# The entry of the down product: two first high parts ahead of a square on ScalarE, and one small load first of four on SyncE's queue

## The reference, cut to what matters

```
u = square(relu(rms_norm(x, g_pre_ffn) @ w_up))      # (T, 1024) @ (1024, 4096)
x = x + rms_norm(u @ w_down, g_post_ffn)             # (T, 4096) @ (4096, 1024)
```

## Time and profile before

| | |
|---|---|
| median of 3 executions | 2371.45 us (2370.8 to 2372.8) |
| the profiled execution's own time | 2372.79 us |
| its span | 2370.2 us |
| mean granted clock of TensorE | 0.998 |
| PE busy | 2341.4 us, 99% |
| DVE busy | 1365.5 us, 58% |
| ACT busy | 797.8 us, 34% |
| POOL busy | 481.4 us, 20% |
| DMA moved | 319.18 MB, mean 135 GB/s |

### The profile page before, as it was taken

One profiled execution on the slowest core, in us unless ns is written; L12 is line 12 of the kernel. 1 busy time (PEld: TensorE's weight loads), 2 busy tenths in 40 slices (PEclk: granted clock), 3 DMA queues, 4 the chain that ended last, 5 costly groups with the idle time before them and its releaser, 6 DMA issues.

```text
span 2370.2 us, 36572 instructions
## 1 busy us (share of the span) xinstructions
PE 2341.4 (99%) x14144; PEld 2198.5 (93%) x14144; DVE 1365.5 (58%) x2494; ACT 797.8 (34%) x1484; POOL 481.4 (20%) x732
## 2 busy tenths in 40 slices
PE   8999999999999999999999999999999999999998
PEld 7899999999999999999999999988999998888886
DVE  7425263553376667667666435556755556777675
ACT  5222223323222232222232423333654554332233
POOL 1002120212165456447536000000000000000001
PEclk9999999999999999999999999999999999999999
DMA  5216363653424324423432644223434336533424
GB/s 194 85 41 229 104 224 114 200 170 125 168 71 135 123 80 132 137 93 112 132 118 88 232 134 132 99 89 98 134 123 154 132 125 253 185 116 125 169 71 142
DMA packets 249990, 319.18 MB, mean 135 GB/s; under 512 B 9332, under 2 KB 191480, under 8 KB 249720
## 3 DMA queue, kind: packets, MB, share of 16 engines
q1 hardware_dynamic: 249416, 315.66, 39.2%
q0 software_dynamic: 432, 1.57, 0.4%
HBM read 205.53 MB, written 111.67 MB: 134 GB/s over the span
## 4 chain that ended last, share of the span: by engine, by line
PE 92%; DVE 5%; POOL 1%; issue 1%; DMA 0%; ACT 0%; DVEq 0%; SPq 0%; POOLq 0%; ACTq 0%
PE bank L935 13%; PE bank L937 13%; PE bank L936 13%; PE bank L1050 5%; PE bank L1049 5%; PE bank L1047 5%; PE bank L1327 5%; PE bank L1329 5%; PE bank L1328 5%; PE bank L1181 1%; PE bank L1009 1%; PE bank L1298 1%; PE bank L1011 1%; PE bank L1010 1%; PE bank L1297 1%; PE bank L1296 1%
## 5 line engine op out<-in xcount | busy, mean ns | idle before, releaser
L935 PE MATMUL bank<-XH,WHI 128*128 128x384 f32 x1968 | 674.2, 343 | 2.3 <-issue 1.5
L937 PE MATMUL bank<-XH,WLO 128*128 128x384 f32 x1968 | 659.3, 335 | 0.0
L936 PE MATMUL bank<-XL,WHI 128*128 128x384 f32 x1968 | 658.8, 335 | 0.0
L935 PEld LDWEIGHTS bank<-XH,WHI 128*128 128x128 f32 x1968 | 370.2, 188 | 6.7 <-issue 3.3
L936 PEld LDWEIGHTS bank<-XL,WHI 128*128 128x128 f32 x1968 | 370.4, 188 | 0.8
L937 PEld LDWEIGHTS bank<-XH,WLO 128*128 128x128 f32 x1968 | 369.9, 188 | 0.0
L1393 ACT ACTIVATE ZST<-bank 128x384 f32<-128x384 f32 x204 | 99.9, 491 | 402.8 <-PE bank L937 396.5
L1327 PE MATMUL bank<-WSH,USH 128*128 128x512 f32 x448 | 175.3, 391 | 2.8 <-DVE USL L2397 2.8
L1329 PE MATMUL bank<-WSH,USL 128*128 128x512 f32 x448 | 175.3, 391 | 0.0
L1328 PE MATMUL bank<-WSL,USH 128*128 128x512 f32 x448 | 175.1, 391 | 0.0
L2546 POOL TENSOR_TENSOR ORS<-OMS,mhalf 128x1 f32<-128x1 f32 x108 | 75.2, 697 | 471.7 <-DVE OMS L2071 471.7
(11 more groups left out here) (282 smaller groups left out, 4807.1 us busy)
## 6 DMA issues: line engine op xcount, KB each, us to landing
WRAW<-in_w_in SPq DMA_DIRECT2D x80, 512.0 KB, 4.1
scratch_z<-ZST SPq DMA_DIRECT2D x68, 576.0 KB, 3.3
UOP<-scratch_uq SPq DMA_DIRECT2D x28, 1024.0 KB, 7.3
HZ<-scratch_z SPq DMA_DIRECT2D x32, 576.0 KB, 4.8
WRAW<-in_w_up SPq DMA_DIRECT2D x32, 512.0 KB, 5.2
scratch_uq<-U SPq DMA_DIRECT2D x16, 1024.0 KB, 3.9
WQ<-in_w_down SPq DMA_DIRECT2D x16, 1024.0 KB, 5.1
scratch_uq<-SU SPq DMA_DIRECT2D x16, 768.0 KB, 5.4
```

Source lines behind the costliest of these rows:

```text
L935: pe.matmul(psum[c][:, 0:CH], WHI[p][:, k, :], XH[:, k, s], start=(k == 0), stop=False)
L936: pe.matmul(psum[c][:, 0:CH], WHI[p][:, k, :], XL[:, k, s], start=False, stop=False)
L937: last = pe.matmul(psum[c][:, 0:CH], WLO[p][:, k, :], XH[:, k, s], start=False, stop=(k == KT - 1))
```

## The change

Two orders are changed, and nothing else: no instruction is added or removed.

- SP: `u8_load(0)` is issued ahead of `wq_load(0, 2)`, `wq_load(0, 3)` and `uq_load(2)`, right after the wait for the end of the up product.
- ACT: in the last step of the up product, `up_sq(s, 1)` (a relu and a square) is issued behind `w_hi_part(0)` and `u_hi(0)` instead of ahead of the wait and of both. In the other steps the order stays.

```
@@ -865,10 +865,10 @@
             uq_load(1)
             uq_store(NQ - 2)
             sp.wait_ge(up_mm, 14 * NP)
+            u8_load(0)
             wq_load(0, 2)
             wq_load(0, 3)
             uq_load(2)
-            u8_load(0)
             uq_store(NQ - 1)
             for n in range(3, 7 * NGD):
                 g, i = divmod(n, 7)
@@ -1834,13 +1834,14 @@
                 if nxt:
                     op_hi(s + 1, 3)
                     op_hi(s + 1, 4)
-                up_sq(s, 1)
                 if nxt:
+                    up_sq(s, 1)
                     op_hi(s + 1, 5)
                 else:
                     act.wait_ge(up_mm, 14 * s + 10)
                     w_hi_part(0)
                     u_hi(0)
+                    up_sq(s, 1)
                 take_last(s, ACT.Relu)
                 up_sq(s, 2)
                 up_sq(s, 3)
```

## The result

| | us | of the kernel before |
|---|---|---|
| before, 22 executions | 2371.89 (2368.84 to 2373.89) | 1 |
| changed, 22 executions | 2375.53 (2373.47 to 2379.04) | 1.0015, 95% interval 1.0010 to 1.0021 |
| predicted | 2371.3 (2368.6 to 2373.8) | |

The change costs 3.6 us, which is within the 0.2% of "the same", but its interval is clear of 1, and the time lies above the predicted range. A longer series than the three executions of before tells smaller differences than the 0.2% that I had put down for a measurement.

What follows compares the result with a forecast made beforehand. PE, busy for 2341.4 of 2370.2 us, bounds the kernel. The gaps' - 1.80 + 1.66 = - 0.14 us gave 2372.65 from the profiled 2372.79; set against the median 2371.45, the forecast was 2371.3 us, range 2368.6 to 2373.8.

Steps and rivals of the forecast that it cites:

- What bounds the entry: At the down product's entry, DVE's unbroken queue behind the squares, not the sample columns' load, sets the 2.0 us second gap.
- ScalarE's part and the first gap: On ACT, WSH starts 1.80 us earlier, the squares' end stays at 1997.95, and PE's first gap is 1.80 us shorter.
- Second gap 3.66 us.: PE's wait for U8L between product 0 and the sample columns grows by 1.66 us, from 2.0 to 3.66.
- Quarter 3 lands at 2004.8 ... I take nothing.: The w_down load, moved past by U8R's, lands 1.4 us later, before DVE's quarter sums want it at 2004.92: cost nothing.
- a cover of 0.12 us: Time between quarter 3's forecast landing at 2004.8 and DVE's quarter sums wanting it at 2004.92.
- Rival 2: At DVE's two quarter sums: quarter 3 is late, + 0.2 us to 2371.65, or 2372.65 with sharing; chance 0.27.
- my 1.4 us for 512 KB: Cost to quarter 3 of U8R's load ahead of it, from two loads landing 2.8 us apart for 1 MB.
- Rival 3: Behind PE's longer second gap the clock falls to half pace: + 2.7 us to 2374.0, 2376.8 at the end; chance 0.07.
- The page's slices give PE the full granted clock everywhere: Reading of the profile page before the change: PE has the full granted clock in all slices.
- the rows of gaps up to 2.8 us show no fall.: In the timeline before the change, PE came out of a 2.8 us gap at full pace, 0.229 us per matmul.

## Why the prediction was wrong, point by point

Two steps failed, both terms that the sum put at nothing: the cost of the earlier load to quarter 3 ("I take nothing"), where DVE waited 1.45 us, and the clock in the longer gap, which cost 2.73 us in the profiles. The clock weighs more: with quarter 3 on time, in the kernel with the load in third place, the median is 2.5 us over before.

- **What bounds the entry.** Right: DVE's queue behind the squares, and not the load of the sample columns. U8H was ready 9 us early and no time was won by it.
- **ScalarE's part and the first gap.** Right in each step: 1.84 us for 1.80, squares' end unmoved, DVE idle for 1.64 us for 1.6, sums 0.03 us behind the last square.
- **"Second gap 3.66 us."** Right as a sum for the kernel without the late quarter: 3.75 in the kernel with the load in third place. In the changed kernel 5.27.
- **"Quarter 3 lands at 2004.8 ... I take nothing."** Wrong. In the changed kernel it lands 11.2 us after the last up matmul, 1.6 later than the 9.6 I had, and DVE waits 1.45 us. With a cover of 0.12 us I took the lower end of a cost whose upper end, 0.34, was itself too low: both were worked out from the spacing of two loads in one execution, and left out whatever else passes through the engines. Rival 2 had the mechanism, a wait of DVE for the load; by its bound of 0.34 us it had a quarter of the price, and its upper price, 1 us more for sharing with the stores, came near the 1.45 us by luck, as holding the stores back changed nothing. The price is not one of SyncE's part alone: with ScalarE's old order the same loads land at 9.7 to 9.8, which needs no wait, and this is what my 1.4 us for 512 KB gives.
- **Rival 3, the clock, at a chance of 0.07.** Wrong in the chance, right in the price in the profiles: 2.7 us forecast, 2.73 in the sum and 2.76 by the kernel with the gap filled (1.5 in its medians). I had the row of slow matmuls at the start, and the rule of the Trainium skill, TensorE: Matmul & The Clock Gate, section HAM oscillation, that a long idle stretch sends the array to half clock; the trace agrees, the granted clock being 0.50 behind the 5.27 us gap. I weighed it down because one profile showed no fall behind 2.80 us. At the entry, gaps of 2.80 us were followed by slow matmuls in two of three profiles, one of 2.58 us in the only one, gaps of 3.75 us and more in all seven, and gaps of up to 2.01 us in none.
- **"The page's slices give PE the full granted clock everywhere", "the rows of gaps up to 2.8 us show no fall."** Misread, and the trace of the kernel before already had the answer. A digit 9 stands for 90% or more, and the mean of 0.998 left room. In the token-mixing part, after a gap of 2.22 us, the clock did fall. The timeline of PE there, then one of the stretches, columns as above:

```profile
677.74 0.33 PE L1142 MATMUL bank<-ident,OT 128*128 128x128 f32 x1 [2.22 <-ACT OT L1599]
...
679.05 0.34 PE L937 MATMUL bank<-XH,WLO 128*128 128x384 f32 x1
...
680.14 0.52 PE L935 MATMUL bank<-XH,WHI 128*128 128x384 f32 x1
...
680.00:682.00 2.00, 2.00 (x8) 2.00 (x7) 2.00 (x6) 0.00 (x0) 1.23 (x1) 0.50 0.16 65
```

  The fall comes 1.5 us behind the gap's end, and 10 matmuls of 384 columns are then 0.32 us apart in place of 0.18. The same gap stands in all 13 profiles of the table and was followed by 5 to 10 such matmuls in eight of them, the changed kernel not among these. So a chance of 0.07 for a gap of 3.66 us had no ground.
- **The sum.** By its own terms - 1.80 + 1.66 = - 0.14. The terms in the profiles are - 1.84, + 1.66 for the gap that only moved (taken from the prediction), + 1.45 for quarter 3, 0.16 that is left over of the measured + 3.27, and + 2.73 for the clock: + 4.16 in the profiles, + 3.6 in the medians.
- **The range** ended at 2373.8, with a scatter added to rival 2 and nothing of rival 3. The two rivals came together: a late load lengthened the gap that the clock fell behind. I had given them apart, as if only one could be.

## What to carry to other kernels

Two gaps on the bounding engine can be one debt: when a step is brought forward and the next one stands on another chain, the first gap's time goes into the second, so follow the releaser of the second gap back until its chain leaves the part that is moved, and change both or neither. Price a longer idle stretch of TensorE with its clock: here 1.84 us won ahead of a wait cost 2.7 behind it. And one profile of a gap in which the clock did not fall is one draw, not a rule: look for the other gaps of the same trace, and at the spacing of the matmuls behind them.

## What the runs showed of the hardware that I had not expected

- **The same gap with and without a fall of the clock.** The gap of 2.22 us above is one case, eight times with and five times without. The first gap, 2.80 us in all of them, was followed by the pace of 0.23 us in the kernel before, and by 7 slow matmuls in each of the two other kernels that have it, from the first on in one and from 1.6 us behind the gap in the other. How many are slow also varies behind like gaps: 13, 8, 6, 8 and 9 behind gaps of 5.2 to 5.3 us.
- **The recorded clock is not always there.** Near the start the same eight matmuls of 384 columns take 2.90 us in both kernels, but the granted clock of that stretch (16 to 20 us) reads 0.50 in the changed kernel:

```profile
16.00:20.00 4.00, 4.00 (x14) 4.00 (x14) 3.65 (x6) 2.74 (x6) 1.98 (x2) 0.50 1.02 402
```

and 1.00 in the kernel before, where the spacing of the matmuls has to tell it:

```profile
16.00:20.00 4.00, 4.00 (x14) 4.00 (x14) 3.33 (x6) 2.77 (x6) 1.98 (x2) 1.00 1.03 405
```

- **A load's landing moves by 1.5 us with an order on another engine.** Between the two kernels with DVE's order changed, ScalarE's order alone moved quarter 3 from 9.7 to 11.2 us, with the same four loads issued at the same times after the last up matmul. What carries it is open; it used up a cover of 0.12 us ten times over.
